# A two-block network on one core: 24 of the 48 modulation blocks beside the first layer's input products, as row sums on VectorE

## The chip, the core and the metric

The kernel runs on one core of a Trainium2 chip. The metric is device microseconds of one execution. PE is the matrix engine TensorE, DVE is VectorE, ACT is ScalarE, POOL is GpSimd, SP is SyncE, whose queue issues the weight transfers. One wait on a semaphore holds everything behind it on its engine.

## The reference, cut to what matters

```python
for l in range(DEPTH):                                   # DEPTH = 2
    sh_l, sc_l, g_l = split(silu(c) @ w_mod[l] + b_mod[l], 3)          # one row, 3 * 2048 numbers
    sh_c, sc_c, g_c = split(silu(c_ctx) @ w_mod[l] + b_mod[l], 3)
    hl = xl * (1 + sc_l) + sh_l                          # 256 tokens x 2048
    hc = xc * (1 + sc_c) + sh_c                          # 256 context tokens x 2048
    parts = split(h @ w_in[l])                           # q, k, v, gates, conv, pool parts
    ... attention in 8 heads, a short convolution, a pool, @ w_out[l], layer norm
second_block(x)                                          # attention, then an MLP
```

The modulation is the product of two condition rows (`silu(c)` and `silu(c_ctx)`) with `w_mod[l]`, a matrix of 2048 x 6144 in each layer: 96 blocks of 1 MB in all, each read once. All arithmetic is in float32.

## The kernel before

Weights are streamed in blocks ("units") of 1 MB, 128 partitions x 2048 numbers, through four places `raw` in SBUF. SP issues all of them in one fixed order (`mod_place`, `weight_place`), each as soon as the block four places earlier has been used. For a unit of ordinary weights ACT rounds each half to fp32r (`w_hi`, L616), DVE subtracts it from the original (`w_lo`, L1123), and PE multiplies three times: hi by hi, hi by rest, lo by hi (L1896 to L1898). A unit of the first layer's input products has 48 such matmuls of 128x512. Both halves of unit n + 2 are rounded while PE works on unit n.

The first layer's input products are the units 12 to 59: four head pairs (p = 0 to 3) of twelve slots each, in the order `IN_SLOTS` = q, k, ag, pu, cu, q, k, ag, cc, cg, pg, cb; the slot is s = (n - 12) mod 12. All of them are accumulated in the same PSUM bank, bank 0, because bank 1 is held by the modulation. So the next unit's product may start only when ACT has evicted the last one to `z` (L629, semaphore `z_full`), and ACT may evict only when DVE has finished with the previous `z` (`z_used`). Behind some products PE has attention work that does not use bank 0: the scores after the ag slots (s = 2 and 7, L2083 and L2089), transposes of the probabilities (after s = 4 and 9), probabilities by values (after s = 5 and 10, L2124), and the transposed output (after s = 6 and 11, L2062).

Of the 96 modulation blocks the first 80 are PE's. 32 go before the stage. 48 (u = 32 to 79) lie beside the 48 units, one ahead of each (`mod_beside`): four small groups of fp32 matmuls, 32 columns of the conditions by 512 columns of raw weights, into bank 1 (L1955). Their raw block stands in the stream right before that of the unit. After every 16 of them, in the units 27, 43 and 59, ACT evicts bank 1 (`take_mod`), PE gathers the sums with four small matmuls halfway through the product (`mod_collect`, L1974), and DVE adds the bias (`later_modulation`). The last 16 blocks are DVE's, in the stage that follows (`gate_products`, L1145).

In each unit ACT does, in order: round half 0 of unit n + 2, evict unit n, perhaps a tanh, round half 1 of unit n + 2, and then what the slot asks for (rounding of q and k, eight exponentials after ag). DVE does: the rest of half 0 of n + 2, perhaps the scaling of the probabilities (s = 3 and 8), wait for `z`, the slot's epilogue, then row maxima or output scaling, the rest of half 1 of n + 2. A wait of PE on the eviction reads:

```python
elif not unit.early(V_UNITS[0] + 1):
    pe.wait_ge(z_full, unit.taken + 1 - unit.back)        # back is 1 in units 12 to 60
```

## Time and profile before

| what | value |
|---|---|
| median of 3 runs | 2925.16 us (2924.89 to 2925.16) |
| the profiled execution | 2924.98 us, of which its span 2923.2 us |
| PE busy | 2897.2 us, 99% |
| DVE busy | 1730.2 us, 59% |
| ACT busy | 1330.8 us, 46% |
| matmuls of the modulation beside units 12 to 59 | 51.1 us of PE in 150 to 785 us of the span |
| granted TensorE clock, mean | 0.998 |

In a timeline row the first number is the start in us from the span's start, the second the duration; the name in front of the arrow is what is written. Ends of matmuls are modelled and overlap the next start, so PE's pace is read from starts. A row may merge several alike instructions (x8); an fp32 matmul shows two records. In brackets stands the idle time of the engine before the row and what ended it.

### The profile page before, as it was taken

The page shows a single profiled execution, that of the slowest core. Times are in us where ns is not written, and L with a number is a line of the kernel's source. Part 1 is how long each engine was busy: PE and PEld are TensorE (multiplying, and loading weights), DVE is VectorE, ACT ScalarE, POOL GpSimd, SP SyncE. Part 2 cuts the span into 40 slices and gives each one's busy share as a digit, 9 for nine tenths or more (in the row PEclk, how much of TensorE's full clock was granted, in tenths as well). Part 3 has the DMA queues.
Part 4 walks back from the last instruction along what each step waited for, and adds up shares of the span by engine and source line. Part 5 has one row for each costly group of instructions (what it writes and reads, how often), then busy time and mean ns, then how long its engine had stood idle before and what let it go on. Part 6 is the DMA issues. An engine that isn't in the chain of part 4 may idle for free.

```text
span 2923.2 us, 42667 instructions
## 1 busy us (share of the span) xinstructions
PE 2897.2 (99%) x15914; PEld 2410.9 (82%) x15914; DVE 1730.2 (59%) x2954; ACT 1330.8 (46%) x2045; POOL 100.3 (3%) x162
## 2 busy tenths in 40 slices
PE   8999999999999999999999999999999999999998
PEld 6777777777788788888887888888888888888887
DVE  3344443434577736666885566667876556565566
ACT  2433333323433535544555545455655445354455
POOL 0000010101000001111000000000000000000000
PEclk9999999999999999999999999999999999999999
DMA  9844343434365324444544444444555555555555
GB/s 380 352 184 162 148 170 145 165 153 169 141 226 213 130 101 148 142 144 145 183 151 166 173 173 159 173 160 172 187 187 202 187 187 190 198 185 190 187 200 188
DMA packets 76378, 527.49 MB, mean 180 GB/s; under 512 B 8864, under 2 KB 11168, under 8 KB 13632
## 3 DMA queue, kind: packets, MB, share of 16 engines
q1 hardware_dynamic: 72448, 513.83, 47.5%
q0 software_dynamic: 2912, 9.57, 0.9%
q8 instruction: 108, 1.77, 0.2%
q10 hardware_dynamic: 864, 1.94, 0.2%
q14 instruction: 46, 0.38, 0.0%
HBM read 523.22 MB, written 2.10 MB: 180 GB/s over the span
## 4 chain that ended last, share of the span: by engine, by line
PE 96%; DVE 1%; DMA 1%; ACT 1%; issue 1%; POOL 0%; POOLq 0%; ACTq 0%; DVEq 0%; SPq 0%
PE bank L1906 27%; PE bank L1909 14%; PE bank L1896 9%; PE bank L1898 9%; PE bank L1897 9%; PE bank L2316 4%; PE bank L2315 4%; PE bank L2317 4%; PE bank L1942 2%; PE bank L1943 2%; PE bank L1944 2%; PE bank L1955 2%; PE bank L2124 1%; DMA raw<-stream 1%; PE bank L2083 1%; PE bank L2008 1%
## 5 line engine op out<-in xcount | busy, mean ns | idle before, releaser
L1123 DVE TENSOR_TENSOR w_lo<-raw,w_hi 128x1024 fp32r<-128x1024 f32 x784 | 949.6, 1225 | 616.7 <-ACT w_hi L616 613.8
L616 ACT ACTIVATE w_hi<-raw 128x1024 fp32r<-128x1024 f32 x784 | 824.2, 1057 | 725.3 <-DMA raw<-stream 286.1
L1896 PE MATMUL bank<-x,w_hi 128*128 128x512 f32 x1120 | 442.5, 395 | 1.2 <-DVE x L1205 1.2
L1898 PE MATMUL bank<-x,w_lo 128*128 128x512 f32 x1120 | 436.4, 390 | 0.0
L1897 PE MATMUL bank<-x,w_hi 128*128 128x512 f32 x1120 | 436.2, 389 | 0.0
L629 ACT ACTIVATE z<-bank 128x512 f32<-128x512 f32 x256 | 153.2, 598 | 461.4 <-PE bank L1909 307.5
L1906 PE MATMUL bank<-xs,w_hi 128*128 128x512 f32 x1184 | 304.7, 397 | 0.0
L1896 PEld LDWEIGHTS bank<-x,w_hi 128*128 128x128 f32 x1120 | 210.2, 188 | 84.2 <-issue 40.9
L1906 PE MATMUL bank<-mlp_x,w_hi 128*128 128x512 f32 x1024 | 257.1, 393 | 0.0
L1898 PEld LDWEIGHTS bank<-x,w_lo 128*128 128x128 f32 x1120 | 210.2, 188 | 44.7
L1906 PEld LDWEIGHTS bank<-xs,w_hi 128*128 128x128 f32 x1184 | 213.0, 189 | 39.9 <-DVE xs L1205 1.1
L1897 PEld LDWEIGHTS bank<-x,w_hi 128*128 128x128 f32 x1120 | 210.4, 188 | 41.9
L1906 PE MATMUL bank<-x,w_hi 128*128 128x512 f32 x896 | 227.9, 396 | 0.3 <-DVE x L1205 0.3
L1906 PEld LDWEIGHTS bank<-mlp_x,w_hi 128*128 128x128 f32 x1024 | 184.3, 189 | 33.1
L2315 PE MATMUL bank<-w_hi,hidden 128*128 128x512 f32 x512 | 199.3, 389 | 0.0
L2316 PE MATMUL bank<-w_lo,hidden 128*128 128x512 f32 x512 | 199.2, 389 | 0.0
L2317 PE MATMUL bank<-w_hi,hidden 128*128 128x512 f32 x512 | 199.2, 389 | 0.0
L1906 PEld LDWEIGHTS bank<-x,w_hi 128*128 128x128 f32 x896 | 161.3, 189 | 33.2 <-issue 2.9
L1909 PEld LDWEIGHTS bank<-xs,w_lo 128*128 128x128 f32 x1184 | 162.0, 190 | 11.6
L1909 PE MATMUL bank<-xs,w_lo 128*128 128x256 f32 x1184 | 166.9, 282 | 0.0
L1909 PEld LDWEIGHTS bank<-mlp_x,w_lo 128*128 128x128 f32 x1024 | 139.7, 190 | 10.0
L1097 DVE TENSOR_TENSOR z<-z 128x256 f32<-128x256 f32 x176 | 74.9, 426 | 121.4 <-ACT z L629 113.5
(341 smaller groups left out, 3510.2 us busy)
## 6 DMA issues: line engine op xcount, KB each, us to landing
raw<-stream SPq DMA_DIRECT2D x488, 1024.0 KB, 4.8
res<-tokens POOLq DMA_DIRECT2D x8, 512.0 KB, 8.9
work<-tokens POOLq DMA_DIRECT2D x16, 256.0 KB, 3.0
out<-res SPq DMA_DIRECT2D x8, 256.0 KB, 2.4
gain_sb<-final_gain ACTq DMA_DIRECT2D x1, 1024.0 KB, 7.5
table_sb<-tables ACTq DMA_DIRECT2D x1, 640.0 KB, 3.5
pool_sb<-pool_w POOLq DMA_DIRECT2D x8, 64.0 KB, 4.2
work<-lam_in POOLq DMA_DIRECT2D x1, 256.0 KB, 9.4
```

Source lines behind the costliest of these rows:

```text
L616: own.inc(act.activation(w_hi[:, 2 * unit.parity + g, :], raw[:, unit.slot, g * HALF:(g + 1) * HALF], ACT.Copy), hi_done, 2 * unit.number ...
L629: last = act.activation(z[:, unit.bank, :], source[:, :], ACT.Copy)
L1097: own.inc_own(dve.tensor_tensor(o, a, b, op))
L1123: own.inc(dve.tensor_tensor(w_lo[:, n, :], raw[:, unit.slot, g * HALF:(g + 1) * HALF], w_hi[:, n, :].bitcast(F32), ALU.subtract), lo_done, ...
L1896: pe.matmul(bank[:, :], hi, tile(k)[:, 0, :], start=k == 0, stop=False)
L1897: pe.matmul(bank[:, :], hi, tile(k)[:, 1, :], start=False, stop=False)
L1898: ins = pe.matmul(bank[:, :], lo, tile(k)[:, 0, :], start=False, stop=k == KT - 1)
L1906: pe.matmul(b[:, :].rearrange("p (a t) -> p a t", a=2), w_hi[:, n, P * kk:P * (kk + 1)], tile(k)[:, :, 0:TOK], start=kk == 0 and (g == 0 o ...
L1909: ins = pe.matmul(b[:, 0:TOK], w_lo[:, n, P * kk:P * (kk + 1)], tile(8 * g + kk)[:, 0, 0:TOK], start=False, stop=kk == KT // 2 - 1 and (g ...
L2315: pe.matmul(bank[:, :], h_hi, hi, start=k == 0, stop=False)
L2316: pe.matmul(bank[:, :], h_hi, lo, start=False, stop=False)
L2317: ins = pe.matmul(bank[:, :], hidden[:, k, 1, P * t:P * (t + 1)], hi, start=False, stop=k == KT - 1)
```

## The change

Of the 48 blocks beside the units 12 to 59, 24 stay with PE (`BESIDE_PE`) and 24 go to DVE (`BESIDE_DVE` = 15, 18, 19, 20, 23 to 27, 30, 31, 32, 35 to 39, 42, 43, 44, 47 to 50). Those of PE are collected in two turns of 12, in the units 40 and 59. Those of DVE (u = 56 to 79, columns of the second layer) are laid out on the host with the output column on the partition and the input row along the free axis. DVE multiplies a 128x512 piece by a row of conditions and sums it in the same instruction (`accum_out`), for both conditions, eight instructions in a block (`share_products`); the products go to the spare half of `z` and are not used. It does so right after its own slot of unit n - 2. For this the conditions must stand in a row on every partition: they are written to DRAM once and read back with a broadcast to all partitions, a quarter (512 numbers) at a time, into two tiles of `res`, four times; SP issues these transfers in between the weights. SP now waits for `share_used` where it waited for `mod_mm` before it reloads the place of a block of DVE's.

```diff
-TURNS = 19
+BESIDE = 3
+TURNS = KT + 2
+SUMMED = 56
...
+TURN_ENDS = [40, 59]
+BESIDE_PE = [12, 13, 14, 16, 17, 21, 22, 28, 29, 33, 34, 40, 41, 45, 46, *range(51, 60)]
+BESIDE_DVE = [n for n in range(PAIRED, PAIRS) if n not in BESIDE_PE]
+ROWS = len(BESIDE_DVE) // 4
...
+        cond_row = [res[:, KT - 2 + s, :] for s in range(2)]
...
+            def load_row(s, q):
+                row = rows_dram[s, 32 * q:32 * (q + 1), :].rearrange("p k -> (p k)")
+                sp.dma_start(cond_row[s], row.partition_broadcast(P)).then_inc(rows_in, 16)
...
+                elif before in mod_at and mod_at[before] >= SUMMED:
+                    done = mod_at[before] - SUMMED + 1
+                    if done % ROWS == 0 and done < 4 * ROWS:
+                        sp.wait_ge(row_used, done // ROWS)
+                        load_row(0, done // ROWS)
+                    sp.wait_ge(share_used, done)
+                    if done % ROWS == 0 and done < 4 * ROWS:
+                        load_row(1, done // ROWS)
                 elif before in mod_at:
                     sp.wait_ge(mod_mm, mod_at[before] + 1)
...
+                if place == RAW_SLOTS - 1:
+                    sp.wait_ge(rows_made, 1)
+                    sp.dma_start(rows_dram.rearrange("s p k -> p s k"), flat_cond).then_inc(rows_out, 16)
+                if place == weight_place(PAIRED - 1):
+                    sp.wait_ge(rows_out, 16)
+                    sp.wait_ge(x_full, KT)
+                    for s in range(2):
+                        load_row(s, 0)
...
+            def share_products(d):
+                place, q, m = mod_place(SUMMED + d), d // ROWS, SUMMED + 4 * (d % ROWS)
+                dve.wait_ge(raw_full[place % RAW_SLOTS], 16 * (place // RAW_SLOTS + 1))
+                if d % ROWS == 0:
+                    dve.wait_ge(rows_in, 32 * (q + 1))
+                own.wait_own()
+                for s in range(2):
+                    for j in range(4):
+                        if s or j:
+                            own.wait_own()
+                        last = dve.scalar_tensor_tensor(out=z[:, 1, :], in0=raw[:, place % RAW_SLOTS, WIDE * j:WIDE * (j + 1)],
+                                                        scalar=1.0, in1=cond_row[s], op0=ALU.mult, op1=ALU.mult,
+                                                        accum_out=part[:, j, s:s + 1])
...
+                own.inc(last, share_used, d + 1)
+                own.wait_own()
+                for s in range(2):
+                    target = mod[:, m:m + 4, s]
+                    start = vec[:, VEC_COLS["b_mod"] + m:VEC_COLS["b_mod"] + m + 4] if q == 0 else target
+                    tt(target, part[:, :, s], start, ALU.add)
...
                     slot(unit, epilogue, before, after, between=first_tiles, late=l == 1, tail=tail)
+                    if l == 0 and unit.fixed + 2 in BESIDE_DVE:
+                        share_products(BESIDE_DVE.index(unit.fixed + 2))
...
             def mod_beside(n):
-                if n < PAIRED:
+                if n not in BESIDE_PE:
                     return None
```

In the order of PE's instructions at the end of unit 17 (s = 5), L1898 is the last of its product, L2124 the probabilities by values, L1955 the modulation block, and then unit 18's product begins. Before:

```order
L1898 MATMUL bank0<-x_52,w_lo_51 128x512
L2124 MATMUL bank5<-res_58,a_t_73 128x128 x12
L1955 MATMUL bank1<-raw_49,cond_x_86 32x512 x4
L1896 MATMUL bank0<-x_52,w_hi_50 128x512
L1897 MATMUL bank0<-x_52,w_hi_50 128x512
```

In the changed kernel, at the same place (its lines are numbered 66 higher; L2191 is the old L2124):

```order
L1964 MATMUL bank0<-x_52,w_lo_51 128x512
L2191 MATMUL bank5<-res_58,a_t_73 128x128 x12
L1962 MATMUL bank0<-x_52,w_hi_50 128x512
L1963 MATMUL bank0<-x_52,w_hi_50 128x512
L1964 MATMUL bank0<-x_52,w_lo_51 128x512
```

The block is gone, and two products into bank 0 follow each other with the attention work alone between them; where a slot has none, nothing is between them.

On DVE, from the epilogue of unit 17 (q) to the start of that of unit 18 (k), before:

```order
L1325 TENSOR_TENSOR q_x<-z,q_x 128x256
L1300 TENSOR_SCALAR work<-bank,tiny 128x128 x4
L1123 TENSOR_TENSOR w_lo<-raw,w_hi 128x1024 x2
L1316 STREAM_SHUFFLE se<-z 128x256
L1097 TENSOR_TENSOR z<-z,rope_sb 128x256
```

and in the changed kernel (L1159 is the old L1123):

```order
L1389 TENSOR_TENSOR q_x<-z,q_x 128x256
L1364 TENSOR_SCALAR work<-bank,tiny 128x128 x4
L1159 TENSOR_TENSOR w_lo<-raw,w_hi 128x1024
L1239 SCALAR_TENSOR_TENSOR z,part<-raw,res 128x512 x8
L1133 TENSOR_TENSOR mod<-part,vec 128x4 x2
L1159 TENSOR_TENSOR w_lo<-raw,w_hi 128x1024
L1380 STREAM_SHUFFLE se<-z 128x256
```

The ten instructions of a block stand between the two rests that followed each other: behind half 1 of unit 19 and ahead of half 0 of unit 20 and of the next epilogue.

On SP, the loads that wait for the blocks and weights of the units 23 and 24 to be used, before:

```order
L473 DMA raw<-stream 128x2048 [waits mod_mm]
L473 DMA raw<-stream 128x2048 [waits lo_done]
L473 DMA raw<-stream 128x2048 [waits mod_mm]
L473 DMA raw<-stream 128x2048 [waits lo_done]
L473 DMA raw<-stream 128x2048 [waits mod_mm]
```

and in the changed kernel, where the rows change for the first time (L495 is `load_row`):

```order
L490 DMA raw<-stream 128x2048 [waits share_used]
L490 DMA raw<-stream 128x2048 [waits lo_done]
L495 DMA res<-cond_rows 128x512 [waits row_used]
L495 DMA res<-cond_rows 128x512 [waits share_used]
L490 DMA raw<-stream 128x2048
L490 DMA raw<-stream 128x2048 [waits lo_done]
```

The two row transfers stand ahead of the next two weight blocks.

## Rows read from the trace of the kernel before

**Rows 1.** The page's part 1: busy us, share of the span, instructions.

```profile
PE 2897.2 (99%) x15914; PEld 2410.9 (82%) x15914; DVE 1730.2 (59%) x2954; ACT 1330.8 (46%) x2045; POOL 100.3 (3%) x162
```

**Rows 2.** Stage sums: window, PE, PEld, DVE, ACT, POOL busy, clock, DMA, GB/s.

```profile
150.00:785.00 635.00, 635.00 (x3162) 485.46 (x3161) 272.33 (x525) 212.30 (x416) 41.29 (x65) 1.00 0.41 160
```

**Rows 3.** Timeline (start us, duration us, engine ...), end of unit 36, all engines.

```profile
482.94 0.39 PE L1898 MATMUL bank<-x,w_lo 128*128 128x512 f32 x1
...
483.26 1.06 PE L1955 MATMUL bank<-raw,cond_x 128*32 128x512 f32 x8
483.36 0.60 ACT L629 ACTIVATE z<-bank 128x512 f32<-128x512 f32 x1 [1.68 <-PE bank L1898]
...
484.25 0.50 PE L1896 MATMUL bank<-x,w_hi 128*128 128x512 f32 x1
```

**Rows 4.** Timeline, PE, end of unit 17, first layer.

```profile
226.62 2.84 PE L2124 MATMUL bank<-res,a_t 128*128 128x128 f32 x24
...
230.38 0.50 PE L1896 MATMUL bank<-x,w_hi 128*128 128x512 f32 x1
```

**Rows 5.** Timeline, PE, the same place in the second layer.

```profile
1110.26 1.95 PE L2124 MATMUL bank<-res,a_t 128*128 128x128 f32 x16
1111.96 0.47 PE L1896 MATMUL bank<-x,w_hi 128*128 128x512 f32 x1
```

**Rows 6.** Timeline, PE, end of unit 14, first layer.

```profile
188.11 1.03 PE L2089 MATMUL bank<-context_k,context_q 64*128 64x256 f32 x8
...
190.06 0.50 PE L1896 MATMUL bank<-x,w_hi 128*128 128x512 f32 x1
```

**Rows 7.** Timeline, PE, the same place in the second layer.

```profile
1128.88 1.65 PE L2083 MATMUL bank<-k_x,q_x 64*128 64x512 f32 x12
1130.46 0.73 PE L1906 MATMUL bank<-x,w_hi 128*128 128x512 f32 x2
```

**Rows 8.** Timeline, PE, end of unit 35.

```profile
470.63 0.60 PE L2062 MATMUL bank<-ident,work 128*128 128x128 f32 x4
...
472.15 0.50 PE L1896 MATMUL bank<-x,w_hi 128*128 128x512 f32 x1
```

**Rows 9.** Timeline, all engines, end of unit 59, the last of the stage.

```profile
792.49 0.60 PE L2062 MATMUL bank<-ident,work 128*128 128x128 f32 x4
792.69 0.60 ACT L629 ACTIVATE z<-bank 128x512 f32<-128x512 f32 x1 [5.28 <-PE bank L1898]
...
793.39 0.47 PE L1896 MATMUL bank<-wide_first,w_hi 128*128 128x512 f32 x1 [0.30 <-issue]
```

**Rows 10.** Timeline, PE, middle of unit 27.

```profile
355.38 0.39 PE L1898 MATMUL bank<-x,w_lo 128*128 128x512 f32 x1
...
356.42 0.49 PE L1896 MATMUL bank<-x,w_hi 128*128 128x512 f32 x1
```

**Rows 11.** Timeline, DVE, four chained scalar_tensor_tensor of the gate products.

```profile
812.30 3.12 DVE L1145 SCALAR_TENSOR_TENSOR work<-raw,cond_x,work 128x512 f32<-128x512 f32 x4
```

**Rows 12.** Groups by form, ACT: busy us, mean ns of one, idle before.

```profile
L792 ACT ACTIVATION_READ_ACCUMULATOR work<-bank 128x1 f32 x48 | 9.3, 194 | 0.0
```

**Rows 13.** Timeline, DVE, units 18 to 20.

```profile
233.87 1.22 DVE L1123 TENSOR_TENSOR w_lo<-raw,w_hi 128x1024 fp32r<-128x1024 f32 x1
...
242.28 0.01 DVE L1316 LOAD_MASK_SELECT se<-z  x1 [2.18 <-ACT z L629]
...
246.33 1.21 DVE L1123 TENSOR_TENSOR w_lo<-raw,w_hi 128x1024 fp32r<-128x1024 f32 x1
...
255.59 0.69 DVE L1145 SCALAR_TENSOR_TENSOR res<-se,z 128x512 f32<-128x512 f32 x1 [1.43 <-ACT se L690]
```

**Rows 14.** Timeline, ACT, unit 20.

```profile
264.98 1.06 ACT L616 ACTIVATE w_hi<-raw 128x1024 fp32r<-128x1024 f32 x1 [2.42 <-DMA raw<-stream]
268.75 0.60 ACT L629 ACTIVATE z<-bank 128x512 f32<-128x512 f32 x1 [2.71 <-PE bank L1898]
```

**Rows 15.** The page's part 6, DMA issues: count, KB each, us to landing.

```profile
cond_sb<-cond ACTq DMA_DIRECT2D x1, 16.0 KB, 5.2
```

More of the change, by code:

```diff
@@ L70, in mod_place @@
         return 5 * (u // 4) + u % 4 + (u % 4 >= 2)
-    return 2 * u - (20 if u < GATED else 19)
+    if u < GATED:
+        return 2 * (BESIDE_PE + BESIDE_DVE)[u - 32] + 20
+    return 2 * u - 19
 def weight_place(n):
@@ L81, in mods_before @@
 def mods_before(turn):
-    return 2 * turn if turn < KT else 32 + 16 * (turn - KT)
+    return 2 * turn if turn < KT else 32 + 4 * BESIDE * (turn - KT)
 def mod_rows(u):
-    turn = u // 2 if u < 32 else KT + (u - 32) // 16
+    turn = u // 2 if u < 32 else KT + (u - 32) // (4 * BESIDE)
     first, last = mods_before(turn), mods_before(turn + 1) - 1
@@ L261, in two_blocks @@
         mix_rms = tiny[:, 56:58]
+        part = place("part", [4, 2])
+        rows_dram = nc.dram_tensor("cond_rows", (2, P, KT), F32, kind="Internal").ap()
+        cond_row = [res[:, KT - 2 + s, :] for s in range(2)]
+        flat_cond = cond_sb[:].rearrange("p k s -> p (k s)").rearrange("p (s k) -> p s k", s=2)
         top = tiny[:, 16:24]
@@ L359, in two_blocks @@
         modz_full = sem("modz_full")
+        rows_made = sem("rows_made")
+        rows_out = sem("rows_out")
+        rows_in = sem("rows_in")
+        row_used = sem("row_used")
+        share_used = sem("share_used")
         mod_sum = sem("mod_sum")
@@ L806, in after @@
                                        qk_rounded, count)
-                        if l == 0 and kind == "ag" and (unit.fixed - PAIRED) % 16 == 14:
-                            act.wait_ge(z_used, unit.taken + 1)
-                            take_mod(KT + (unit.fixed - PAIRED) // 16, 1, 1)
                         if kind == "ag":
@@ L821, in after @@
                                 late_tile(k)
-                    if l == 0 and (unit.fixed - PAIRED) % 16 == 15 and s != 3:
-                        take_mod(KT + (unit.fixed - PAIRED) // 16, 1, 1)
+                    if l == 0 and unit.fixed in TURN_ENDS:
+                        act.wait_ge(share_used, sum(n < unit.fixed for n in BESIDE_DVE))
+                        take_mod(KT + TURN_ENDS.index(unit.fixed), 1, 1)
                     def rest_of_operand():
@@ L1402, in tail @@
                                 late_rest(k)
-                    if l == 0 and (unit.fixed - PAIRED) % 16 == 15:
+                    if l == 0 and unit.fixed in TURN_ENDS:
                         inner = before
                         def before():
-                            later_modulation(KT + (unit.fixed - PAIRED) // 16)
+                            later_modulation(KT + TURN_ENDS.index(unit.fixed))
                             inner()
@@ L1978, in mod_beside @@
             def mod_beside(n):
-                if n < PAIRED:
+                if n not in BESIDE_PE:
                     return None
-                turn = KT + (n - PAIRED) // 16
+                u = 32 + BESIDE_PE.index(n)
+                turn, _, first, last = mod_rows(u)
                 if n == PAIRED:
                     pe.wait_ge(v_out, 7)
-                elif (n - PAIRED) % 16 == 0:
+                elif u == first:
                     pe.wait_ge(mod_done, turn)
-                mod_product(20 + n, 1)
-                if (n - PAIRED) % 16 == 15:
+                mod_product(u, 1)
+                if u == last:
                     return lambda: mod_collect(turn, 1, 1)
@@ L2401, in weight_stream @@
     early = a["w_mod"][0][:, :2 * D].reshape(KT, P, 2, KT, P).transpose(3, 2, 1, 0, 4).reshape(-1, P, UNIT)
-    mods = np.concatenate([early, first[32:], second])
+    w = a["w_mod"][1][:, (SUMMED - NMOD) * P:(GATED - NMOD) * P]
+    w = w.reshape(KT, 4, 32, ROWS, 4, P).transpose(1, 3, 5, 4, 2, 0).reshape(-1, P, UNIT)
+    mods = np.concatenate([early, first[32:], second[:SUMMED - NMOD], w, second[GATED - NMOD:]])
     parts = [in_order(a["w_in"][0], True), units_of(mixer_rows(a["w_out"][0], False)),
```

11 lines of the change are left out of this document (9 added, 2 removed).

## The prediction, made before the changed kernel ran

> **What bounds the kernel now.** I read the page's busy line first: PE is busy for 99% of the span, DVE for 59%, ACT for 46% [rows 1]. Then the sums of the stage in which the 48 blocks lie, 150 to 785 us: PE 635.00 us of 635.00, DVE 272.33, DMA engines 0.41 busy, clock 1.00 [rows 2]. In this stretch PE is never idle, so a microsecond taken from PE is won if nothing else is late in its place, and a microsecond given to DVE is free as long as what PE waits for still comes in time. The third view is the timeline at the ends of units, since there the blocks stand and there PE depends on ACT and DVE. One block is about 1.06 us of PE [rows 3], so 24 of them look like 25 us. That is not the gain, because a block also does a second service: it covers the eviction of bank 0.
>
> **What a removed block gives, by its place.** Starts are compared, since ends overlap. There are three kinds of places.
>
> *Behind q and k (s = 0 and 1), nothing else covers.* These are the blocks of the units 25, 26, 37, 38, 49, 50. The last matmul starts at 482.94, ACT evicts from 483.36 to 483.96, the block runs from 483.26, and the next product starts at 484.25 [rows 3]. Without the block it starts when the eviction is done. What that takes is seen at unit 60, the one place before which PE has no block and bank 0 is alone: the eviction ends at 793.29 and PE starts at 793.39, 0.10 later [rows 9]. So 483.96 + 0.10 = 484.06 in place of 484.25: 0.19 us a block, 6 x 0.19 = 1.1 us.
>
> *Behind a transposed output (s = 6 and 11): units 19, 24, 31, 36, 43, 48.* From the start of the transposes to the next product it is 472.15 - 470.63 = 1.52 us with the block [rows 8], and 793.39 - 792.49 = 0.90 without it, at unit 60, where the eviction again decides [rows 9]. 6 x 0.62 = 3.7 us.
>
> *Behind longer attention work, the eviction is long done: 12 blocks.* Six follow the probabilities by values (18, 23, 30, 35, 42, 47). There the work's end (226.62 + 2.84 = 229.46) to the next product (230.38) is 0.92 us [rows 4]; in the second layer, with no block, the product starts 0.25 us before the modelled end (1112.21 against 1111.96) [rows 5]. 1.17 us each, 7.0 us. Six follow the scores (15, 20, 27, 32, 39, 44): 190.06 against an end of 189.14, 0.92 [rows 6]; without a block 1130.46 against 1130.53, -0.07 [rows 7]. 0.99 us each, 5.9 us. Here the two layers' last matmuls differ in shape, so this is the looser pair.
>
> *One turn less.* Three collections become two. In the middle of a product one stretches the step from one matmul's start to the next to 356.42 - 355.38 = 1.04 us [rows 10]. The step without it is something between nothing and the 0.39 us that one matmul is shown with, so it costs 0.65 to 1.04; I take 0.8. That the others now end in unit 40 and not in 43 changes nothing: ACT and DVE do the same work one slot kind later, and the next turn starts in unit 41 behind it as it did in 44.
>
> Sum of PE: 1.1 + 3.7 + 7.0 + 5.9 + 0.8 = 18.5 us.
>
> **What is put on DVE.** One block is eight scalar_tensor_tensor of 128x512 that wait for each other, and two additions of 128x4. The nearest row is the gate products: the same operation, raw weights with SBUF, four in a chain in 3.12 us, 0.78 each [rows 11]. The reading out of the sum is not in any DVE row; on ACT such a read takes 194 ns and lies partly under its neighbours [rows 12]. From below the read is free, 8 x 0.78 = 6.2 us; from above it is in full, 8 x 0.97 = 7.8, and some 0.3 us for the two additions (an estimate). I take 0.1 a read, 8 x 0.88 = 7.0 and 0.2: 7.2 us. 24 blocks are 173 us, and DVE in this stretch goes from 272 to about 445 of some 617 us: 72%. On the average it fits. The question is the bunches, since half of each head pair's blocks follow each other directly.
>
> *The bunch 18, 19, 20, worked in the trace's times.* DVE ends the rest of half 1 of unit 19 at 233.87 + 1.22 = 235.1 [rows 13]. Block 19 goes to 242.3, the rest of half 0 of unit 20 (1.22) to 243.5. Before, the epilogue of unit 18 began at 242.28 [rows 13]; PE is by now 1.2 us earlier, so it would like to begin at 241.1, and is 2.4 late. Nobody waits: k is needed by the scores a whole product later. This slot's work took until 246.33 + 1.21 = 247.5, 5.3 us [rows 13], now until 248.8; block 20 to 256.0; the rest to 257.2. The epilogue of unit 19 began at 255.59 [rows 13] and is now at 257.2, 1.6 us later in absolute time. Behind it stand the maxima, behind those ACT's exponentials. ACT had ended them at 264.98 - 2.42 = 262.56, then waited for a weight block [rows 14]. Now 262.56 + 1.6 = 264.2, and 1.06 for rounding gives 265.2. The eviction of unit 20 was at 268.75 [rows 14]; PE is 1.2 + 0.6 + 1.0 = 2.8 earlier, so PE wants it at 265.9. ACT is ready 0.7 us ahead. **The cover is there, but it is thin:** with 7.2 us a block nothing is lost, and each 0.1 us more on a block moves this by 0.2. The bunch 23 to 27 is five long, with more room per unit (two of its slots have short epilogues); by the same steps ACT is some 2 us ahead at its end at 7.2 us, and loses 0.5 for each 0.1 us more.
>
> *The transfers.* SP now waits for `share_used` where it waited for PE. In the worst case above block 20 is used up at 256.0, and unit 20's product, 2.8 us earlier than before, begins about then too, which is when PE would have used it; so the weights behind it are not issued much later. The rows are 256 KB each, eight times; with the DMA engines at 0.41 [rows 2] they add under 1 us ahead of a weight block at three places, while the rounding has about that much room. The first two are issued once the last tile of x is made, and the next block's place comes free only with the rests of unit 8, which DVE does after that tile, so they hold nothing up. At the start SP writes the conditions to DRAM, 16 KB; a like one was 5.2 us under way, with nobody of the stream behind it but the issue [rows 15]. For all this I take 0.5 us, between 0 and 3.
>
> The sum: 18.5 - 0.5 = 18.0 us off the profiled execution's 2924.98 us, 2907.0. The median is 0.18 above that, so **2907.1 us**.
>
> **Rivals.** *A: the eviction was hidden, so little comes free.* It would hold if the places behind attention work gave no more than those behind q and k, for instance because two kinds of matmul behind each other cost what the block did. Then it is 24 x 0.19 + 0.8 = 5.4 us, 2919.8. Against it are [rows 5, 7, 9], which show the places without a block. *B: a block on DVE takes 7.8 to 8.3 us.* Then ACT is late at the ends of the bunches: 2 x 0.9 - 0.7 = 1.1 us in three bunches of the first kind, and 5 x 0.9 - 2 = 2.5 in three of the second at 8.1 us, together 11 us, and 2918; DVE catches up while PE waits, so it is rather less, 2912 to 2918. For it is the unknown read. *C: the sums run at half the pace.* If a scalar_tensor_tensor with two fp32 operands in SBUF and a sum takes two cycles an element, each of the eight is longer by that part of its 0.78 us that goes with the elements, about 0.53 us (an estimate), so a block is 7.2 + 4.2 = 11.4 us. A head pair has 12 units in about 155 us, DVE work of about 68 us and seven or eight blocks, 86 us, with the waits for ACT and POOL inside: DVE is the bound. In the five-long bunch DVE falls back by 4.2 us a block more, 21 less the 2 of room; PE then waits some 10 us in each of three pairs and 5 in each short bunch. 18 - 45 = 27 us slower, 2952; it decides from about 9 us a block, where the gain is used up. The row speaks against it as far as it goes: such an operation without a sum takes 0.78 us [rows 11], which is no half pace. *D: the change does not move the work off PE's path*: the instruction order shows it does, no chance.
>
> The Trainium skill, "Vector Engine (DVE) Microarchitecture Reference", section "Points that are easy to get wrong", says that a scalar_tensor_tensor with two SBUF sources that are not bf16 halves throughput, since both read ports are in use and none is left to read back the accumulator. That is rival C; by that rule the kernel comes out slower, and no row of this trace has the form with a sum. The page "VectorE: DVE Perf Modes", section "Two Vector instructions with no wait between them", says that an operation which writes out its accumulator is two instructions; this is the read priced above.
>
> **How the numbers follow.** Forecast 0.66, with 2903 to 2911 for it (the read free and no transfers late, or 4 us of small stalls). B 0.15, A 0.07, C 0.09, and 0.03 for something slow that I do not see. A measurement of this kernel tells about 0.2%, 5.9 us, from no change. Faster by more: the forecast, B, and what of A comes out a little better: 0.83. Within: the rest of A and of the unseen, 0.07. Slower: C and a part of the unseen, 0.10. The range is 2902 to 2919, which holds the forecast, B and a part of A.
>
> **What would show it.** In the changed kernel's profile: the eight-fold group of share instructions at 0.69 to 0.8 us each and a small read behind each; over 1.1 us is C. At the ends of units without a block the product starts 0.1 us after the eviction behind q and k, and directly behind the attention work elsewhere. PE idle ahead of L1962 (the old L1896) some 0.1 to 0.3 us at 12 places and nothing above; idle of 1 us or more ahead of unit 21 or 28 is B. ACT's eviction of unit 20 follows PE by 0.4 us as before, or is held by the exponentials. DVE near 445 us busy in the stage. Wrong would be also a stage that is shorter by 18 us with a kernel that is not: then something behind the stage has grown.

## The result, and the profile after

The changed kernel takes 2906.49 us (median of 4 runs, 2905.47 to 2907.48), the kernel before, on the same chip, 2925.07 us (median of 4, 2924.89 to 2925.16). The ratio is 0.9937, with a 95% interval of 0.9919 to 0.9954: faster by 18.6 us. Predicted were 2907.1 us, with a range of 2902 to 2919. The profiled execution of the changed kernel took 2907.48 us with a span of 2905.8; that of before took 2924.98 with 2923.2. The spans differ by 17.4 us.

The page of the changed kernel, busy us, share of the span and instructions, answers to [rows 1]:

```profile
PE 2870.5 (99%) x15714; PEld 2405.7 (83%) x15714; DVE 1867.9 (64%) x3385; ACT 1330.1 (46%) x2044; POOL 99.1 (3%) x162
```

Its sums over the stage of the blocks answer to [rows 2]. Columns: window, its length, PE, PEld, DVE, ACT, POOL busy, granted clock, DMA share, GB/s:

```profile
150.00:768.00 618.00, 611.81 (x2974) 482.43 (x2973) 412.85 (x957) 213.55 (x417) 40.18 (x65) 1.00 0.44 168
```

DVE has gone from 272.33 us in 635 to 412.85 in 618, and PE, which was never idle, is now idle for 618.00 - 611.81 = 6.2 us. The list of PE's waits from 140 to 820 us says where (line, releaser, us in total, times, longest):

```profile
PE bank L1962 <- issue: 3.5, 9, 0.7
PE bank L1962 <- DVE w_lo L1159: 2.9, 4, 0.7
```

These are 13 waits of 0.7 or 0.3 us ahead of a unit's first matmul, all that the list has of this stage. The longest is 0.7, so nothing has been late by a microsecond anywhere in the stage. The releasers are inferred, and neither name is what PE waits for: at all these places the first matmul of the next unit starts 0.10 us after the eviction of bank 0 has ended, as the following rows show.

**The four kinds of places.** All four groups are timelines of the changed kernel: start, duration, engine, line, operation, and in brackets the idle time before it. First the end of unit 36, behind q, which answers to [rows 3]:

```profile
473.78 0.39 PE L1964 MATMUL bank<-x,w_lo 128*128 128x512 f32 x1
474.20 0.60 ACT L667 ACTIVATE z<-bank 128x512 f32<-128x512 f32 x1 [2.07 <-PE bank L1964]
...
474.90 0.47 PE L1962 MATMUL bank<-x,w_hi 128*128 128x512 f32 x1 [0.73 <-issue]
```

The last product's matmul starts at 473.78 and the next unit's at 474.90. That is 1.12 us, where it was 484.25 - 482.94 = 1.31 with the block [rows 3]: 0.19 us. PE starts 0.10 us after the eviction's end (474.20 + 0.60 = 474.80), and it is idle for 0.73 us in between, since nothing covers the eviction any more. Then the end of unit 35, behind a transposed output, which answers to [rows 8]:

```profile
462.11 0.60 PE L2129 MATMUL bank<-ident,work 128*128 128x128 f32 x4
462.30 0.60 ACT L667 ACTIVATE z<-bank 128x512 f32<-128x512 f32 x1 [4.32 <-PE bank L1964]
...
463.00 0.47 PE L1962 MATMUL bank<-x,w_hi 128*128 128x512 f32 x1 [0.30 <-issue]
```

From the transposes' last group at 462.11 to the next product at 463.00 it is 0.89 us, where it was 1.52 [rows 8]: 0.63 us. Here too the eviction decides (462.30 + 0.60 + 0.10 = 463.00). Then the end of unit 17, behind the probabilities by values, as [rows 4], and that of unit 14, behind the scores, as [rows 6]:

```profile
229.39 2.84 PE L2191 MATMUL bank<-res,a_t 128*128 128x128 f32 x24
231.98 0.48 PE L1962 MATMUL bank<-x,w_hi 128*128 128x512 f32 x1
```

```profile
191.89 1.02 PE L2156 MATMUL bank<-context_k,context_q 64*128 64x256 f32 x8
192.85 0.50 PE L1962 MATMUL bank<-x,w_hi 128*128 128x512 f32 x1
```

From start to start these are 2.59 and 0.96 us, where they were 3.76 [rows 4] and 1.95 [rows 6]: 1.17 and 0.99 us. PE goes from the attention work straight into the next product, without a gap.

**The block on DVE.** The line of the new operation: duration min/median/max in ns, first and last start, form and count:

```profile
L1239 DVE SCALAR_TENSOR_TENSOR z<-raw,res x192: 691/691/695, 183.8 to 638.9; 128x512 f32<-128x512 f32 x192
L1239 DVE DVE_READ_ACCUMULATOR z<-raw,res x192: 80/81/86, 184.4 to 639.5; 128x1 f32 x192
```

Eight times 24 are 192, and each takes 691 ns. The timeline of DVE shows the end of block 19 and the first and the last rows of block 20:

```profile
243.08 0.69 DVE L1239 SCALAR_TENSOR_TENSOR z<-raw,res 128x512 f32<-128x512 f32 x1
243.70 0.08 DVE L1239 DVE_READ_ACCUMULATOR z<-raw,res 128x1 f32 x1
243.82 0.24 DVE L1133 TENSOR_TENSOR mod<-part,vec 128x4 f32<-128x4 f32 x2
...
250.68 0.69 DVE L1239 SCALAR_TENSOR_TENSOR z<-raw,res 128x512 f32<-128x512 f32 x1
...
256.55 0.24 DVE L1133 TENSOR_TENSOR mod<-part,vec 128x4 f32<-128x4 f32 x2
```

A sum of 0.69 us begins at 243.08 and its read at 243.70, before it has ended. Block 20 goes from 250.68 to 256.55 + 0.24 = 256.79: **6.1 us**, of which the additions are 0.24, and the eight pairs 5.87, 0.735 each. The prediction had 7.2 us.

### The profile page after: what moved, and what is told of

Its sections match the earlier page's. It is cut to its first block, busy times and chain, and to the rows that moved or that the text cites. A ratio compares the mean times of both kernels' runs of the same rounds, so it can differ in the third digit from the quotient of the medians.

```text
span 2905.8 us, 42731 instructions
## 1 busy us (share of the span) xinstructions
PE 2870.5 (99%) x15714; PEld 2405.7 (83%) x15714; DVE 1867.9 (64%) x3385; ACT 1330.1 (46%) x2044; POOL 99.1 (3%) x162
## 3 DMA queue, kind: packets, MB, share of 16 engines
q0 software_dynamic: 2912, 9.57, 0.9%
## 4 chain that ended last, share of the span: by engine, by line
PE 94%; DVE 2%; DMA 1%; ACT 1%; issue 1%; POOL 0%; SPq 0%; POOLq 0%; ACTq 0%; DVEq 0%
PE bank L1972 27%; PE bank L1975 14%; PE bank L1962 9%; PE bank L1964 9%; PE bank L1963 9%; PE bank L2382 4%; PE bank L2383 4%; PE bank L2384 4%; PE bank L2008 2%; PE bank L2010 2%; PE bank L2009 2%; PE bank L2191 1%; DMA raw<-stream 1%; PE bank L2150 1%; PE bank L2075 1%; DVE w_lo L1159 1%
## 5 line engine op out<-in xcount | busy, mean ns | idle before, releaser
L1159 DVE TENSOR_TENSOR w_lo<-raw,w_hi 128x1024 fp32r<-128x1024 f32 x784 | 949.0, 1224 | 473.2 <-ACT w_hi L654 470.3
```

The lines of the kernel that those rows point to most:

```text
L1159: own.inc(dve.tensor_tensor(w_lo[:, n, :], raw[:, unit.slot, g * HALF:(g + 1) * HALF], w_hi[:, n, :].bitcast(F32), ALU.subtract), lo_done, ...
```

## Where the 17.4 us of the two profiled executions lie

I compared the start of the same matmul in the two traces. At the beginning of the stage the changed kernel is **3.8 us later** than before (the product of unit 12 starts at 155.07 and not at 151.29). At the end of the stage it is 15.8 us earlier (unit 60's starts at 777.55 and not at 793.39), so the stage went from 642.10 to 622.48 us and gave 19.6; forecast were 18.5. Behind the stage another 1.6 us came, all of it in one place of the second layer's norm. -3.8 + 19.6 + 1.6 = 17.4.

The 3.8 us arise for the most part between 34 and 50 us, long before the first changed block. PE waits there for a weight block from HBM. The row is shown of before and then of the changed kernel:

```profile
35.74 1.08 PE L1965 MATMUL bank<-raw,cond_x 128*32 128x128 f32 x32 [1.29 <-DMA raw<-stream]
```

```profile
36.49 1.94 PE L2031 MATMUL bank<-raw,cond_x 128*32 128x128 f32 x32 [1.95 <-DMA raw<-stream]
```

PE's wait is 1.95 us in place of 1.29, and the block starts 0.75 us later. The window from 35 to 50 us follows, first of before, then of the changed kernel (columns as above), and behind them the part of the latter with the low clock:

```profile
35.00:50.00 15.00, 14.26 (x162) 11.50 (x166) 4.41 (x13) 4.98 (x8) 0.53 (x1) 1.00 0.97 395
```

```profile
35.00:50.00 15.00, 13.51 (x131) 10.83 (x132) 2.66 (x8) 3.26 (x5) 0.53 (x1) 0.77 0.73 281
35.76:42.58 6.82, 6.09 (x42) 4.75 (x43) 0.00 (x0) 0.38 (x1) 0.00 (x0) 0.50 1.02 410
```

The granted clock stands ahead of the last two numbers: 1.00 before, 0.77 after. From 35.76 to 42.58 us it was at 0.50, the lower of its two levels, and for 6.09 us of that PE had matmuls, at half their pace: 3.0 us lost. The block's later start of 0.75 us makes 3.8 of it. The change does add something near here: SP waits for `rows_made` and writes the conditions to DRAM. Whether this caused it was the first question to the chip (e1). Behind the stage, the norm's stretch shows a low clock too, in both kernels, that of before and then that of after:

```profile
1508.00:1520.00 12.00, 11.30 (x47) 7.02 (x46) 7.01 (x26) 4.58 (x10) 0.69 (x1) 0.72 0.26 88
```

```profile
1492.00:1504.00 12.00, 11.03 (x54) 7.22 (x53) 7.61 (x27) 5.06 (x11) 0.69 (x1) 0.86 0.23 89
```

The mean clock was 0.72 before and 0.86 after: it stood at 0.50 for 6.8 us before and for 3.4 after, and half the difference is 1.7 us, about the 1.6. The change has no instruction there.

## The experiments

The theory, call it **P**, is the prediction's sum: what the change gains is what PE's places give (0.19, 0.62, 1.17 or 0.99 us by what stands ahead of them), and DVE's work costs nothing as long as ACT's eviction keeps its lead. The rivals: **W**, that the write to DRAM holds the beginning up; **D**, that DVE's work already costs something in the changed kernel; **E**, that a block is worth about the same everywhere, so that only the count of blocks matters. Each kernel below was timed beside the kernel before on the same chip; the diffs are against the changed kernel.

### e1: the write of the conditions moved away from the beginning

```diff
                 load(place, place % RAW_SLOTS)
-                if place == RAW_SLOTS - 1:
+                if place == weight_place(PAIRED - 3):
                     sp.wait_ge(rows_made, 1)
                     sp.dma_start(rows_dram.rearrange("s p k -> p s k"), flat_cond).then_inc(rows_out, 16)
```

> Moves one DMA of the changed kernel: the conditions go to DRAM some 110 us later, ahead of the last two units of the value stage, and not at 7.5 us. The profiled execution of the changed kernel reached the first input product 3.8 us later than the kernel before, with the granted clock at 0.50 from 36 to 42 us. Theory W: the write at the start delays the transfers that PE waits for there. Then the stage begins 3 to 4 us earlier, at 147 us or before, and the time is 2903 us, 3 below the changed kernel. Rival N: the write has nothing to do with it, and how the transfers of the weights and tokens fall in the first 40 us varies from execution to execution with PE being a little earlier; then the time is 2905 to 2907 and executions differ by 1 to 2 us as those of the changed kernel do.

Measured: 2905.89 us (5 runs, 2905.49 to 2908.19) against 2924.89, ratio 0.9935 [0.9921, 0.9948]. Against the changed kernel's 2906.49 that is nothing that can be told. Its window from 35 to 50 us:

```profile
35.00:50.00 15.00, 13.55 (x139) 10.98 (x140) 4.03 (x10) 3.29 (x5) 0.53 (x1) 0.89 0.80 324
```

The clock is down here as well, at 0.89, with no write at this place. And e4 below has the write where the changed kernel has it, and shows none of it:

```profile
35.00:50.00 15.00, 14.26 (x158) 11.46 (x162) 4.50 (x14) 4.94 (x8) 0.53 (x1) 1.00 0.97 391
```

Nor is the start of the stage tied to the write: unit 12's product begins at 154.5 us in e1, without the write at this place, and at 151.0 in e8 below, with it (before: 151.3). So W falls. The loss at the beginning comes and goes between executions, with and without the write. It is one reason why the profiled spans differ by less than the stage gave.

### e2: two sums in place of eight

This kernel leaves six of the eight sums of each block out, so its modulation values are incomplete; all else is issued as before.

```diff
+            own.inc_own(dve.memset(part[:], 0.0))
...
                 for s in range(2):
-                    for j in range(4):
-                        if s or j:
+                    for j in (3,):
+                        if s:
                             own.wait_own()
```

> Leaves out six of the eight sums of each block on DVE (the modulation of the second layer's last 24 columns blocks is then incomplete), all else as in the changed kernel: a block on DVE is some 1.7 us and not 6.1. Theory: DVE's work is hidden entirely, so the time is that of the changed kernel, 2906 within 1 us. Rival: the sums cost PE something through late evictions; then it is 2 to 6 us faster.

Measured: 2906.87 us (4 runs, 2905.37 to 2908.09), ratio 0.9937 [0.9922, 0.9953]. The stage's window:

```profile
150.00:768.00 618.00, 611.81 (x2973) 482.41 (x2972) 313.54 (x669) 212.89 (x417) 40.28 (x65) 1.00 0.43 168
```

DVE does 99 us less than in the changed kernel (313.54 against 412.85), and PE's 611.81 us are the same to the hundredth. So is the stage: from the start of unit 12's product to that of unit 60's it is 622.48 us in the changed kernel, in e1 and in e2. DVE's work was hidden entirely; D falls at this size.

### e5, e6 and e3: ten, twelve and sixteen sums a block

Here sums are issued twice, so a block on DVE costs more, and its result is the same. One line decides how many:

```diff
+                        for again in range(int(j == 0)):
+                            own.inc_own(dve.scalar_tensor_tensor(out=z[:, 1, :], in0=raw[:, place % RAW_SLOTS, WIDE * j:WIDE * (j + 1)],
+                                                                 scalar=1.0, in1=cond_row[s], op0=ALU.mult, op1=ALU.mult,
+                                                                 accum_out=part[:, j, s:s + 1]))
+                            own.wait_own()
                         last = dve.scalar_tensor_tensor(out=z[:, 1, :], in0=raw[:, place % RAW_SLOTS, WIDE * j:WIDE * (j + 1)],
```

This is e5. In e6 the range is `range(j % 2)`, in e3 `range(1)`.

> Each sum of a block is made twice, 16 instructions and 12.0 us a block in place of 6.1: what it would be if the form ran at half pace. By the cover worked out from the trace (ACT is ready 2.7 us ahead of the eviction of unit 20 at 6.1 us a block, and each us more on a block takes 2 of it in a bunch of three and up to 5 in a bunch of five) PE waits about 9 us at the end of each of three short bunches and 10 to 20 in each of three long ones: 2940 to 2975, slower than the kernel before. Rival: the bunches even out over a head pair, and the stage is bound by DVE's sum only, 445 + 140 us against 618, so not at all: 2906 to 2912.

> Two of the eight sums of each block on DVE are made twice: 7.6 us a block and not 6.1, all else as in the changed kernel. In its trace ACT sat idle 2.7 us before the evictions of the units 20 and 44 and 1.2 before that of 32. Theory (two blocks of a short bunch stand ahead of the exponentials, so each us on a block takes 2 of that): 3.0 us of the 2.7 are taken, 0.3 to 1.8 us lost at three places, and little in the bunches of five, which had 4.2 us: 2907 to 2911. Rival: the cover is larger than the idle time shows, since ACT could have done its rounding earlier; 2906, no change.

> Four of the eight sums of each block are made twice: 9.1 us a block. With sixteen, 12.0 us a block, the kernel was 88 us slower, of which some 7 us each time were PE waiting behind the scores of a head and some 2 more the granted clock at 0.50 behind that wait. Theory: the loss begins near 7.4 us a block and goes with the length of a bunch, so 9.1 us cost 3.3 to 5 us at each of three short bunches and 5 to 9 at each of three long ones, and 1 to 2 of clock each time: 2931 to 2950. The mere load of DVE (272 + 218 of 618 us, 79%) would say no loss: 2906.

Measured (the price of a block is so many sums times their pitch of 0.735 us, and 0.24; in the traces a block takes 1.70, 6.11, 7.58, 9.05 and 11.98 us from its first start to its last end):

| kernel | sums | block on DVE, us | median, us | ratio to before, 95% | DVE busy, 150 to 768 |
|---|---|---|---|---|---|
| e2 | 2 | 1.7 | 2906.87 | 0.9937 [0.9922, 0.9953] | 313.54 |
| changed kernel | 8 | 6.1 | 2906.49 | 0.9937 [0.9919, 0.9954] | 412.85 |
| e5 | 10 | 7.6 | 2908.84 | 0.9941 [0.9925, 0.9956] | 447.92 |
| e6 | 12 | 9.1 | 2937.81 | 1.0045 [1.0029, 1.0060] | 469.28 |
| e3 | 16 | 12.0 | 2994.27 | 1.0234 [1.0219, 1.0250] | 508.08 |

(The window of e6 and e3 holds less of the stage, since theirs is longer.) PE's waits from 140 to 820 us in e5, e6 and e3, in this order:

```profile
PE bank L1967 <- issue: 8.9, 14, 2.0
```

```profile
PE bank L1967 <- issue: 28.2, 19, 4.7
```

```profile
PE bank L1967 <- issue: 57.5, 20, 8.3
```

At 7.6 us a block little happens; at 9.1 the gain is gone and 12 us with it; at 12.0 it is 69. The stage itself, from unit 12's product to unit 60's, tells more finely than the medians: 622.48 us with 8 sums, 624.99 with 10, 652.04 with 12 and 712.73 with 16.

**e5.** The median came within what was expected, and the stage is 2.5 us longer than the changed kernel's. The loss isn't where it was expected, though. All of it lies ahead of two products, 0.45 us at unit 25 and 2.06 at unit 33, and nothing at the units 21 and 45. ACT's timeline ahead of unit 33:

```profile
424.73 1.06 ACT L654 ACTIVATE w_hi<-raw 128x1024 fp32r<-128x1024 f32 x1 [2.03 <-DMA raw<-stream]
425.69 0.58 ACT L667 ACTIVATE z<-bank 128x512 f32<-128x512 f32 x1
```

The last matmul of unit 32 started at 422.98, so bank 0 could have been evicted from 423.4 on. ACT had ended its exponentials at 422.7, but then waited 2.03 us for a weight block, rounded it, and only then evicted. So it was not held by DVE's maxima, as the expectation has it, but by a transfer. Both places lie where SP first waits for DVE to use up a block (24 and 32) and then issues two row transfers ahead of the weights; the change has three such points, and these are the first two. That DVE's lateness and the rows together made it late is inferred from this order; no run has the one without the other.

**e6 and e3.** e6 came within what was expected. e3 did not: 2940 to 2975 was expected and 2994 measured. Its worst places show why. ACT's timeline, behind the bunch 18, 19, 20:

```profile
272.02 0.69 ACT L782 ACTIVATE work<-bank,tiny 128x512 f32<-128x512 f32 x1 [11.80 <-DVE tiny L1451]
...
276.74 1.07 ACT L654 ACTIVATE w_hi<-raw 128x1024 fp32r<-128x1024 f32 x1
277.69 0.61 ACT L667 ACTIVATE z<-bank 128x512 f32<-128x512 f32 x1
```

ACT waits 11.80 us for DVE's maxima, ends its exponentials and the next rounding, and only at 277.69 evicts bank 0. PE's product had ended long ago:

```profile
270.76 1.07 PE L2026 MATMUL bank<-raw,cond_x 128*32 128x512 f32 x8
278.39 0.77 PE L1967 MATMUL bank<-x,w_hi 128*128 128x512 f32 x1 [6.57 <-issue]
...
279.38 0.63 PE L1969 MATMUL bank<-x,w_lo 128*128 128x512 f32 x1
279.81 0.63 PE L1967 MATMUL bank<-x,w_hi 128*128 128x512 f32 x1
```

PE starts 0.1 us after the eviction (278.39 against 277.69 + 0.61 = 278.30), having been idle for 6.57 us. And behind the wait it runs on slowly. Three windows of 2 us:

```profile
276.00:278.00 2.00, 0.00 (x0) 0.00 (x0) 0.26 (x2) 2.00 (x6) 0.00 (x0) 0.61 1.11 381
278.00:280.00 2.00, 1.61 (x4) 1.36 (x5) 1.93 (x5) 1.24 (x2) 0.00 (x0) 0.50 0.93 381
280.00:282.00 2.00, 2.00 (x7) 1.54 (x6) 1.93 (x6) 0.00 (x0) 0.00 (x0) 0.50 0.14 57
```

The granted clock falls to 0.50 during the idle time and is still there when PE has work again: the matmuls follow each other by 0.43 us (279.38 to 279.81), where it is 0.23 in the changed kernel. It is at full speed again some 5 us after PE's start (0.68 in the window from 282 to 284, 1.00 in the next), so a long wait costs about 2.4 us more than its length. This second cost stood in none of the expectations written before e3 ran; that of e6, written after it, has it. Its sum can be read. Between unit 12 and unit 60 the clock of e3 was at 0.50 in 14 stretches. Their sum (length, PE, PEld, DVE, ACT, POOL busy, and the means):

```profile
sum 75.09, PE 56.36 PEld 45.31 DVE 62.52 ACT 32.36 POOL 0.00; mean PE 4.03 PEld 3.24 DVE 4.47 ACT 2.31 POOL 0.00
```

PE had matmuls in 56.4 of these 75.1 us, at half pace, which is 28.2 us lost. PE's waits from 140 to 820 us hold 63 more than in the changed kernel: 57.5 ahead of L1967 and 11.8 ahead of the scores, less 6.4. Together that is 91, and the stage is 90.3 us longer (712.73 - 622.48). The same sum for e6: 28.2 - 6.4 = 21.8 us of waits, and five stretches at 0.50 with 16.2 us of matmuls, 8.1 lost; together 29.9, where the stage is 29.6 longer. So waits and clock are the whole of the loss in both.

### e4: other places, the same number of blocks

In the changed kernel six of DVE's blocks stood behind q and k (25, 26, 37, 38, 49, 50), where a removed block gave 0.19 us. e4 gives these back to PE and takes 17, 22, 29, 34, 46 and 51 instead, whose evictions other work covers.

```diff
-BESIDE_PE = [12, 13, 14, 16, 17, 21, 22, 28, 29, 33, 34, 40, 41, 45, 46, *range(51, 60)]
+BESIDE_PE = [12, 13, 14, 16, 21, 25, 26, 28, 33, 37, 38, 40, 41, 45, 49, 50, *range(52, 60)]
```

> Still 24 blocks on DVE, but others: the six behind q and k (25, 26, 37, 38, 49, 50) and 41 wait... are PE's again together with 41, and DVE takes 17, 22, 29, 34, 46, 51 instead, which stand behind attention work, so that only blocks of the kinds worth 0.63 to 1.2 us are moved. Theory (what a block gives is what stands above the eviction): the sum by place goes from 17.9 to about 23.7 us, 5.8 us faster than the changed kernel, 2900.5. Rival: a block gives PE the same wherever it stands; then 2906, no change. Second rival: DVE is too full in the slots behind s = 3 and 8, where the probabilities are scaled, and the gain is lost in late evictions: 2903 to 2910.

Unit 41, which the expectation names with these, is PE's in both kernels. Measured: 2900.66 us (5 runs, 2899.21 to 2901.88), ratio 0.9917 [0.9904, 0.9931]. That is 5.8 us below the changed kernel, and it beats both; by the stage alone it is 5.77 us (616.71 against 622.48), and 5.8 were expected. (The intervals of the two ratios overlap, 0.9904 to 0.9931 against 0.9919 to 0.9954. The runs don't: 2899.21 to 2901.88 against 2905.37 to 2908.19 of e1 and e2, which ran on the same chip as e4 and differ from the changed kernel in nothing that PE sees.) The count of blocks is the same, so E can't explain it. The end of unit 21 in the changed kernel, with block 22 on PE, and then in e4:

```profile
280.50 1.03 PE L2164 MATMUL bank<-ident,work 128*128 128x128 f32 x8
...
282.76 1.07 PE L2021 MATMUL bank<-raw,cond_x 128*32 128x512 f32 x8
283.76 0.50 PE L1962 MATMUL bank<-x,w_hi 128*128 128x512 f32 x1
284.10 0.40 PE L1963 MATMUL bank<-x,w_hi 128*128 128x512 f32 x1
```

```profile
277.02 1.03 PE L2164 MATMUL bank<-ident,work 128*128 128x128 f32 x8
...
278.79 0.79 PE L1962 MATMUL bank<-x,w_hi 128*128 128x512 f32 x1
279.42 0.40 PE L1963 MATMUL bank<-x,w_hi 128*128 128x512 f32 x1
```

From the transposes to the next product's first matmul it was 3.26 us and is 1.77. That difference of 1.49 us is too large a price for the block, though: in e4 the first matmul is shown to start early and the second follows 0.63 us behind it, where it is 0.34 in the changed kernel, and the product of unit 22 is then longer by as much. To the second matmul it was 284.10 - 280.50 = 3.60 us and is 279.42 - 277.02 = 2.40: 1.20 us from one block, six times what one behind q gives. PE's idle places are gone as well: seven waits of 0.3 us are left.

```profile
PE bank L1962 <- issue: 2.1, 7, 0.3
```

### e7 and e8: twelve blocks, badly and well placed

The sharpest test of E. Both kernels move 12 blocks, keep 36 on PE and have three turns with a collection each, as before; they differ only in which units' blocks DVE has.

```diff
-TURNS = KT + 2
-SUMMED = 56
+TURNS = KT + 3
+SUMMED = 68
...
-TURN_ENDS = [40, 59]
-BESIDE_PE = [12, 13, 14, 16, 17, 21, 22, 28, 29, 33, 34, 40, 41, 45, 46, *range(51, 60)]
+TURN_ENDS = [29, 45, 59]
+BESIDE_PE = [n for n in range(12, 60) if n not in (14, 16, 21, 25, 26, 28, 33, 37, 38, 40, 49, 50)]
```

This is e7: at each of these twelve places only the block covers the eviction. In e8 the turns end at 28, 46 and 59 and DVE has 15, 18, 20, 23, 27, 30, 32, 35, 39, 42, 44 and 51, all behind attention work.

> Only 12 blocks go to DVE, and only such as stand ahead of units behind which PE has nothing but the eviction (14, 16, 21, 25, 26, 28, 33, 37, 38, 40, 49, 50); PE keeps 36, in three turns as before. Theory (a block there is worth what it stands above the eviction, 0.19 us): 12 x 0.19 = 2.3 us, so 2922.7. Rival (a block is worth its own 1.0 to 1.06 us on PE wherever it stands): 12.4 us, 2912.6.

> The counterpart: 12 blocks go to DVE, all behind attention work of PE that is longer than the eviction (15, 18, 20, 23, 27, 30, 32, 35, 39, 42, 44, 51), PE keeps 36 in three turns. Theory: five at 1.17 and seven at 1.00 us, 12.9 us, so 2912.1. Rival (the same wherever it stands): then as its counterpart.

Measured: e7 2923.61 us (11 runs, 2922.14 to 2925.47), ratio 0.9992 [0.9983, 1.0002]; e8 2912.68 us (5 runs, 2909.68 to 2912.89), ratio 0.9954 [0.9941, 0.9968]; the kernel before 2925.77 on this chip. **The same twelve blocks fewer on PE give nothing that can be told in one, and 13 us in the other.** They are 10.9 us apart, where the sum of their places gives 10.6 (2922.7 and 2912.1). The stage, 642.10 us before, is 639.54 in e7 and 628.82 in e8: 2.6 and 13.3 us shorter, where 2.3 and 12.9 were forecast for the places. PE's waits of e7 and then of e8, 140 to 820 us:

```profile
PE bank L1962 <- DVE w_lo L1159: 6.6, 9, 0.7
PE bank L1962 <- issue: 2.5, 4, 0.7
```

```profile
PE bank L1962 <- issue: 0.3, 1, 0.3
```

In e7 13 waits, 9.1 us in all: twelve bare evictions of 0.7 us and unit 60's of 0.3. In e8 only unit 60's is left. In e7 the block was taken away and the eviction took its place on PE's path. E falls; and with it rival A of the prediction, which would have given e8 no more than e7.

## Why the prediction was right, and which terms were not

**The bound.** PE was the bound of the stage, and a microsecond taken from it was won: shown by e2, where DVE's share changes by 99 us and nothing else does, and by e4, e7 and e8.

**The places.** 0.19, 0.62, 1.17 and 0.99 us were forecast from pairs of rows, three of them from the second layer or from unit 60; the changed kernel's rows give 0.19, 0.63, 1.17 and 0.99 to 1.00. The pair of the scores, called the looser one, was as good as the others. Their sum is 6 x 0.19 + 6 x 0.63 + 6 x 1.17 + 6 x 1.0 = 17.9.

**One turn less.** Forecast 0.8. Unit 27, whose collection is gone, is 0.97 us shorter from the start of its product to that of the next. Read in the same way, from product to product, the places give slightly more than the single steps above: 0.20 to 0.21 us behind q and k, 0.67 to 0.71 behind the transposed outputs, 1.16 to 1.18 behind the probabilities by values and 0.99 to 1.03 behind the scores, 18.5 in all. With the collection and some 0.15 us spread over other units this is the stage's 19.6.

**The block on DVE.** This is the mis-sized term: 7.2 us forecast, 6.1 measured. The pitch of 0.78 was from the gate products [rows 11], whose scalar is a column of SBUF: they take 0.752 us each, 0.788 apart. The new operation has the constant 1.0 and takes 0.691 us. The read was priced at 0.1 on top of the pitch and is 0.08 us, but lies mostly under its neighbours: with it, the sums are 0.735 apart. Blocks of 7.2 us should have left DVE at 445 us in the stage, and it has 412.85. The error stayed almost without effect, as the next term shows.

**The thin cover at unit 20.** Forecast was that ACT would be ready 0.7 us ahead of the eviction. It was 2.66:

```profile
268.60 0.60 ACT L667 ACTIVATE z<-bank 128x512 f32<-128x512 f32 x1 [2.66 <-PE bank L1964]
```

The difference of 2.0 us is two blocks 1.1 us cheaper each, which is just what the prediction said a block's price would do there (0.2 for each 0.1 us). The statement "with 7.2 us nothing is lost" was about right for this bunch: e5, with 7.6 us, loses nothing at unit 21. The prediction worked the bunch of 23 to 27 more roughly and took the other short ones for like the first, which they were not. At unit 32 ACT's idle time ahead of the eviction is 1.21 us in the changed kernel and not 2.66, since ACT waits 1.37 us for a weight block first, and at unit 24 it is 0.91. Two blocks 1.1 us dearer each would have used that up, so at the forecast price about 1 us would have been lost (an estimate from these numbers); e5 lost 2.5.

**The transfers and the beginning.** Forecast 0.5 us, 0 to 3. e1 shows that the write costs nothing that can be told. The rows (256 KB each) came without holding anything that PE waits for in the changed kernel, but the two thin places just named, at the units 24 and 32, are those behind row transfers, and they are where e5 lost its time. The page's line on them, 4.4 us each to landing:

```profile
res<-cond_rows SPq DMA_DIRECT2D x8, 256.0 KB, 4.4
```

**The rivals.** A fell (e7 against e8). B, a block of 7.8 to 8.3 us, was not the case; e5 at 7.6 and e6 at 9.1 stand on both sides of it, and say 2909 and 2938, so B's 2912 to 2918 at 8.1 us lies between them; no run had that price. B's mechanism, ACT late behind its exponentials, is seen in e3, but the first loss, in e5, came by a weight block. C, half the pace, fell in one row: 691 ns for a 128x512 of two fp32 operands in SBUF with a sum, where the same size without a sum takes 0.69 too [rows 13]. The Trainium skill's rule behind C ("Vector Engine (DVE) Microarchitecture Reference", section "Points that are easy to get wrong") is not what these rows show. The Trainium skill's page "VectorE: DVE Perf Modes", section "Two Vector instructions with no wait between them", is borne out: the operation with a sum comes as two instructions, 192 and 192. C's threshold, "about 9 us a block, where the gain is used up", was right (e6, 9.1 us, is 12 us slower, so it lies a little below); C's size was not. It gave 27 us slower at 11.4 us, and e3 at 12.0 is 69 us slower. The clock that falls behind each long wait (28 us in e3) was left out there; PE's waits for the scores' operands (11.8 us) were too. How much more the backlog of one bunch weighed on the next was not measured apart.

**What would show it.** Most signs came as said: 0.69 us and a small read, PE 0.10 us behind the eviction, ACT's eviction 0.4 us behind PE. One was off: PE's idle time at the twelve bare places was given as 0.1 to 0.3 us, and six of them have 0.73. The step from start to start was right, but without the block there is nothing on PE for the whole of the eviction, and the sign should have been 0.3 behind transposes and 0.7 behind q and k.

**The total.** 2907.1 forecast and 2906.49 measured. Some of that closeness is luck: the stage gave 1.1 us more than forecast, no transfer took the 0.5 us set aside for it, and the median carries whatever clock the beginning and the norms happened to have (in the profiled execution -3.8 and +1.6 us). The mechanism doesn't hang on that luck, since the stage by itself went from 642.10 to 622.48 us.

## What to carry to other kernels

A piece of filler work on the bounding engine is worth its length only where something else already covers what it covered. Before moving it, find for each place the step from the last useful instruction to the next one with and without it; here that ranged from 0.19 to 1.20 us for the same 1.06 us of work, and choosing the places by it gave nearly a third more than the change did (24.2 us against 18.6). Compare the second matmul behind the gap as well as the first, whose start can be shown too early.

An engine with spare time on the average takes work at no cost until the first place where something that the bound engine waits for comes late, and that can be a transfer which its work releases. Here 6.1 us a block cost nothing (DVE 67% busy in the window), 7.6 cost 2.5 us (72%), and 9.1 cost 30 (76%). Past that point most of the added work is lost: from 7.6 to 9.1 us the 24 blocks grow by 35 us in all and the stage by 27, from 9.1 to 12.0 by 70 and 61.

## What the runs showed of the hardware

- A `scalar_tensor_tensor` of 128x512 fp32 with a sum takes 691 ns, as without one; the read of the sum is an instruction of 81 ns, of which 44 ns show in the pitch (735 ns).
- The same operation with a column of SBUF as its scalar takes 752 ns in the gate products, and 691 with a constant.
- TensorE's granted clock fell to 0.50 (1.2 GHz) behind idle times of 1.95 and 6.57 us and stayed there for some microseconds of work.
- In the wait for a weight block near 35 us, the clock fell in the changed kernel, e1, e2 and e5, after 1.78 to 2.20 us of idle time, and stayed at 1.00 in before, e3, e4, e7 and e8, after 1.29 to 1.55, but also in e6 after 2.07. It cost 3.0 us in the changed kernel, and 1.7 in e1, e2 and e5. In the first layer's norm it fell for 3.4 us or more in e1 to e5 and e7, and not in the other four, without an idle time of PE over 0.5 us ahead of it. The kernel before ran in 2922.78 to 2929.49 us over 15 runs on one chip.
- PE starts 0.09 to 0.10 us after an eviction ends, at all places looked at, also with the clock at 0.50. The eviction of a 128x512 bank takes 0.60 us and starts 0.42 us after the start of the last matmul.
